# Turned first triangular blocks on VectorE instead of through HBM, and an earlier block store

## The chip, the core and the metric

The kernel runs on one NeuronCore of a Trainium2 chip. TensorE (PE in the profile) does the matrix products, VectorE (DVE) and ScalarE (ACT) the element-wise work, GpSimd (POOL) small work and some DMA, and SyncE (SP) streams the weights. The metric is the device time of one launch, in microseconds (us), lower is better; the median over several runs counts.

## What is computed

One layer of a bidirectional encoder for 256 tokens of width 2048, in float32: a SwiGLU feed-forward, then two mixers side by side (a bidirectional RWKV-7 recurrence and differential attention) that gates merge, then a second feed-forward. The parts that matter here:

```python
proj = u @ w_in[i]
rw_seg, q, k, v, gate_a, gate_b = jnp.split(proj, col_split, axis=-1)
y_a = rwkv7_branch(rw_seg, ...)        # a scan over time, both directions
y_b = diff_attention_branch(q, k, v, ...)
merged = jax.nn.sigmoid(gate_a) * (y_a @ w_branch_a[i]) + jax.nn.sigmoid(gate_b) * (y_b @ w_branch_b[i])

def step(S, inp):                      # the scan of rwkv7_branch
    sa = -jnp.einsum('dbhij,dbhj->dbhi', S, kk_t)
    S = S * w_t[..., None, :] + sa[..., :, None] * (kk_t * a_t)[..., None, :] + v_t[..., :, None] * k_t[..., None, :]
    return S, jnp.einsum('dbhij,dbhj->dbhi', S, r_t)
```

The kernel runs the scan in chunks of 64 tokens. Each chunk needs the inverse of a unit triangular 64x64 matrix, `z`. There are 128 such matrices (16 heads, 2 directions, 4 chunks).

## The kernel before

**Slots.** Every large product is cut into slots. A slot is 512 KB of weights (256 rows by 512 columns). SP loads it to `raw`, ACT rounds it to `whi` (L534), DVE makes the remainder `wlo` (L1031), and PE multiplies it in 12 matmuls of 512 columns (L1667 to L1669). The ring has 4 places. ACT may write slot n only when PE has finished slot n-4, and SP may load slot n only when DVE is done with slot n-4.

**The gate stage.** The gates' product has 64 slots, k = 0 to 63, and other work is woven into it by hand: each engine has its own list of what it does after which slot. On ACT and DVE the list runs four slots ahead of PE's, since these engines prepare slots that PE reaches later. So what DVE does after `wlo` of slot 54 belongs to the time in which PE is at slot 50 or 51. The woven work is the attention (scores on PE, `maxima` on DVE, `exps` on ACT, `maps` on DVE, transposed maps and products with the values on PE, `squares` on ACT, `head_squares` and `norm_heads` on DVE, transposed heads on PE, `store_heads` from POOL) and the triangular inverses. `S_AT` says after which slot of PE the scores of attention step n come, n = 0 to 7, and the numbers in brackets below are these n, or the group g = 0 to 3 of two steps.

**The inverses.** DVE inverts the two 32x32 diagonal blocks of all 128 matrices by elimination in `z`, where a partition holds a matrix (`step`, L1394 and L1396), in the gaps of slots up to about the 42nd. POOL stores `z` to HBM (`z_dram`, L2338) and reads it back in four groups g of 16 chunks as `zs`, where a partition holds a row of the matrices (`load_z`, L2325). The remaining block is the product of the first diagonal block with the off-diagonal one and the second diagonal block: PE does `vz_products(g)` (L1935) after slot 51 + 2g and `z12_products(g)` (L1943) after slot 52 + 2g, and ACT moves the results (L825, L833). The stationary operand of `vz_products` is `z1t`, the first diagonal block turned over. Before, DVE wrote the turned blocks to `zt` (L1398), POOL stored them (L2340) and read them back in the other layout (L2344).

**POOL's queue** is one list in order: a wait in it holds all that stands behind it. `rms(1)` waits for DVE, `store_heads(1)` for ACT's copy of the heads, `load_z(g)` for PE to have used slot 45 + 2g.

Of the kernel before, what the change touches and what calls it, by code (L numbers as in the profile page):

```python
# [38 lines left out]
ALU = mybir.AluOpType  # L39
# [3 lines left out]
P = 128  # L43
# [6 lines left out]
RING = 4  # L50
# [5 lines left out]
RW = 1024  # L56
# [7 lines left out]
C = 64  # L64
NC_ = T // C
HC = C // 2
NM = 2 * NPAIR
# [46 lines left out]
def layer(nc, a, out):  # L114
# [85 lines left out]
    def scratch(name, shape):  # L200
        return nc.dram_tensor(name, shape, F32).ap()
# [8 lines left out]
    z_dram = scratch("z_dram", (2, NM, NC_, C, C))  # L210
    beta_dram = scratch("beta_dram", (P, NM, T))
    yt_dram = scratch("yt_dram", (P, 8, T))
    z1t_dram = scratch("z1t_dram", (2, NM, NC_, HC, HC))

    ctx = ExitStack()
    with ctx:
        def sem(name):
            return ctx.enter_context(nc.semaphore(name))

        def sb(scope, name, shape, dt=F32):  # L220
            return scope.enter_context(nc.sbuf_tensor(name, shape, dt))
# [14 lines left out]
        def room(*names):  # L236

            scope = ExitStack()
            tiles = [sb(scope, *n) for n in names]
            return scope, tiles  # L240
# [9 lines left out]
        def ffn_room(tag):  # L250
# [28 lines left out]
        s_e.close()  # L279
        s_rk.close()  # L280

        s_z, (z, zt, ra, rb, xin, mx, su, os_, _, gst_g, yts) = room(
            ("z", [P, C + 1, C]), ("zt", [P, HC * HC]), ("ra", [P, RW]), ("rb", [P, RW]), ("xin", [P, 4, RW]),
            ("mx", [P, 2, 2]), ("su", [P, 2, 2]), ("os_", [P, 16]), ("z_gap", [P, 168]),
            ("gst_g", [P, 2, NT, CW]), ("yts", [P, 4, P]))
        qk = [xin[:, i, :].rearrange("p (n t) -> p n t", t=P) for i in range(4)]
# [50 lines left out]
        bon_in, bon_mm, bon_st, bon_out, v1_in = (sem(n) for n in ("bon_in", "bon_mm", "bon_st", "bon_out", "v1_in"))  # L337
        n_mm, n_st, z_in, z_done, z_out = (sem(n) for n in ("n_mm", "n_st", "z_in", "z_done", "z_out"))
        n_out = [sem("n_out0"), sem("n_out1")]
        z1t_out, z1t_in, vz_mm, vz_ready, z12_mm, z12_ready = (  # L340
            sem(n) for n in ("z1t_out", "z1t_in", "vz_mm", "vz_ready", "z12_mm", "z12_ready"))
        ZG = 4
        xin_in = zs_in = [sem(f"xin_zs_in{g}") for g in range(ZG)]
        ZS_LANDED = 16 + 32
        PER_ZG = NM * NC_ // ZG
        GATE_SLOTS = p_gate.chunks * p_gate.slots
        Z_FIRST, Z_LAST, ZS_AT, VZ_AT, Z12_AT, ZG_STEP = 13, 41, 46, 51, 52, 2
# [669 lines left out]
        def _(dve):  # L1017
            links = [0]

            def link(ins):  # L1020
                links[0] += 1
                ins.then_inc(dve_link, 1)
                dve.wait_ge(dve_link, links[0])

            V = nc.vector

            def split_lo(p):
                def slot(n, i, u, j):
                    s = slot_of(p, u, j)
                    dve.wait_ge(hi_ready, n + 1)  # L1030
                    V.tensor_tensor(wlo[:, s, :, 0:p.width], raw[:, s, :, 0:p.width],  # L1031
                                    whi[:, s, :, 0:p.width].bitcast(F32), ALU.subtract).then_inc(lo_ready, 1)
                return slot
# [243 lines left out]
            for c in range(7):  # L1277
# [3 lines left out]
                for i in range(4 if c < 6 else 0):  # L1281
# [7 lines left out]
                    if c == 1 and i == 3:  # L1289
                        dve.wait_ge(lora_act, GS_SPLIT + 2)  # L1290
                        r = slice(32, 64)
# [89 lines left out]
            def steps_by(k):  # L1381

                share = min(max(k - Z_FIRST, 0) / (Z_LAST - Z_FIRST), 1)
                return next(i for i in range(HC + 1) if sum(STEP_WORK[:i]) >= share * sum(STEP_WORK) - 1)

            def step(s):
                n = HC - 1 - s
                if s == 0:
                    dve.wait_ge(z_in, 16)
                    link(V.memset(ones, 1.0))  # L1390
                elif n:
                    prod = ra[:, 0:2 * s * n].rearrange("p (k c t) -> p k c t", k=2, c=s)
                    rest = zd[:, :, 0:s, s + 1:HC]
                    link(V.tensor_tensor(prod, zd[:, :, 0:s, s:s + 1].broadcast_to((P, 2, s, n)),  # L1394
                                         zd[:, :, s:s + 1, s + 1:HC].broadcast_to((P, 2, s, n)), ALU.mult))
                    link(V.tensor_tensor(rest, rest, prod, ALU.add))  # L1396
                else:
                    V.tensor_copy(zt[:, :].rearrange("p (t c) -> p t c", c=HC),  # L1398
                                  z[:, 0:HC, 0:HC].rearrange("p c t -> p t c")).then_inc(z_done, 1)

            def ends(m):

                if m >= 2:
                    dve.wait_ge(gh_mm, 2 * (m - 1))
                at = 1 + 3 * NC_ * NM + NC_ * (m % 2)
                V.tensor_tensor(q[:, at:at + NC_, :], q[:, 0:1, scan_columns(m)].broadcast_to((P, NC_, C)),
                                pend[:, m, :].unsqueeze(2).broadcast_to((P, NC_, C)), ALU.mult).then_inc(dd_ready, 1)

            def maxima(n):

                dve.wait_ge(sc_mm, n + 1)
                for s in range(2):
                    last = V.tensor_reduce(mx[:, :, s], ps[:, 4 + s, :].rearrange("p (v t) -> p v t", v=2), AX.X, ALU.max)
                link(last)
                V.tensor_scalar(mx[:, :, :], mx[:, :, :], -0.125, None, ALU.mult).then_inc(mx_ready, 1)
# [16 lines left out]
            def head_squares(g):  # L1432
                dve.wait_ge(pv_sq, g + 1)
                V.tensor_scalar(os_[:, 4:8], os_[:, 0:4], 1.0 / P, SUBLN_EPS, ALU.mult, ALU.add).then_inc(pv_ms, 1)

            def norm_heads(g):
                dve.wait_ge(pv_rs, g + 1)
                V.tensor_tensor(ov[:, :, :], ps[:, 6, :].rearrange("p (v i) -> p v i", v=4),
                                os_[:, 8:12].unsqueeze(2).broadcast_to((P, 4, P)), ALU.mult).then_inc(yb_ready, 1)

            slots = p_gate.chunks * p_gate.slots
            for k in range(slots):
                if k == slots - 2:
                    dve.wait_ge(z12_mm, ZG)
                    ends(0)
                    ends(1)
                if k >= RING:
                    split_lo(p_gate)(p_gate.n0 + k, 0, k // p_gate.slots, k % p_gate.slots)
                if k in TURN_AT:
                    i = TURN_AT.index(k)  # L1450
                    dve.wait_ge(xin_in[i], 16)
                    rope(V, xin[:, i, :], i % NT, ra[:, :], rb[:, :], roped, i, dve)
                for n in range(8):
                    if k - RING == S_AT[n]:
                        maxima(n)
                    if k - RING == S_AT[n] + 2:
                        maps(n)
                    if n % 2 and k - RING == S_AT[n] + PV_LATE:
                        head_squares(n // 2)
                    if n % 2 and k - RING == S_AT[n] + PV_LATE + 1:  # L1460
                        norm_heads(n // 2)
                for s in range(steps_by(k), steps_by(k + 1)):
                    step(s)

# [193 lines left out]
        def _(pe):  # L1658
# [265 lines left out]
            def vz_products(g):  # L1924
                if g == 0:
                    pe.wait_ge(n_st, NM)
                    pe.wait_ge(z1t_in, 32)
                    pe.wait_ge(qk_turned, 4)
                pe.wait_ge(zs_in[g], ZS_LANDED)
                if g:  # L1930
                    pe.wait_ge(z12_ready, g)
                for j in range(PER_ZG):
                    for h in range(2):
                        a_, b_, mc = slice(C * h, C * h + HC), slice(C * h + HC, C * (h + 1)), PER_ZG * g + j
                        last = mm(ps[b_, 7, j * HC:(j + 1) * HC], zs[a_, mc, HC:C], z1t[a_, mc, :], start=True, stop=True)  # L1935
                last.then_inc(vz_mm, 1)
# [248 lines left out]
        def _(pool):  # L2185
# [3 lines left out]
            def link(ins):  # L2189
                links[0] += 1  # L2190
                ins.then_inc(pool_link, 1)
                pool.wait_ge(pool_link, links[0])
# [123 lines left out]
            def store_heads(g):  # L2316
                hs, t = 4 * (g % 2), g // 2
                pool.wait_ge(yb_out, g + 1)
                pool.dma_start(yt_dram[:, hs:hs + 4, t * P:(t + 1) * P], yts[:, :, :]).then_inc(yt_out, 16)

            def load_z(g):
                pool.wait_ge(slots_used, p_gate.n0 + ZS_AT + ZG_STEP * g)
                ms = slice(NM // ZG * g, NM // ZG * (g + 1))
                for h in range(2):
# [8 lines left out]
            store_heads(0)  # L2333
            store_gates([3])
            rms(1)
            store_heads(1)
            pool.wait_ge(z_done, 1)
            pool.dma_start(z_dram.rearrange("h m c s t -> (h m c) (s t)"),  # L2338
                           z[:, 0:C, :].rearrange("p c t -> p (c t)")).then_inc(z_out, 16)
            pool.dma_start(z1t_dram.rearrange("h m c s t -> (h m c) (s t)"), zt[:, :]).then_inc(z1t_out, 16)  # L2340
            store_gates([4])
            pool.wait_ge(z1t_out, 16)
            for h in range(2):
                pool.dma_start(z1t[C * h:C * h + HC, :, :], z1t_dram[h].rearrange("m c s t -> s (m c) t")).then_inc(z1t_in, 16)  # L2344
            pool.wait_ge(z_out, 16)
            load_z(0)
            load_z(1)
# [106 lines left out]
```

## Time and profile before

| | us |
|---|---|
| median of 3 runs | 2337.79 (2337.22 to 2338.06) |
| time of the profiled execution | 2336.86 |
| its span, first to last instruction | 2335.1 |
| PE busy | 2303.0 (99%) |
| DVE busy | 1503.2 (64%) |
| ACT busy | 1119.6 (48%) |
| DMA, mean over the span | 193 GB/s |

PE is the engine that decides, so the table is read as: what does PE wait for, and how long. All times below are us from the start of the span. The gate stage's last third, in which the inverses lie, runs from about 1196 to 1296.

### The profile page before, as it was taken

The page shows a single profiled execution, that of the slowest core. Times are in us where ns is not written, and L with a number is a line of the kernel's source. Part 1 is how long each engine was busy: PE and PEld are TensorE (multiplying, and loading weights), DVE is VectorE, ACT ScalarE, POOL GpSimd, SP SyncE. Part 2 cuts the span into 40 slices and gives each one's busy share as a digit, 9 for nine tenths or more (in the row PEclk, how much of TensorE's full clock was granted, in tenths as well). Part 3 has the DMA queues.
Part 4 walks back from the last instruction along what each step waited for, and adds up shares of the span by engine and source line. Part 5 has one row for each costly group of instructions (what it writes and reads, how often), then busy time and mean ns, then how long its engine had stood idle before and what let it go on. Part 6 is the DMA issues. An engine that isn't in the chain of part 4 may idle for free.

```text
span 2335.1 us, 32570 instructions
## 1 busy us (share of the span) xinstructions
PE 2303.0 (99%) x12207; PEld 1883.9 (81%) x12207; DVE 1503.2 (64%) x2022; ACT 1119.6 (48%) x1504; POOL 133.5 (6%) x209
## 2 busy tenths in 40 slices
PE   9999999999999999999999999999999999999998
PEld 7888888888887778777887877887888888888886
DVE  5766754566756665997974556756676665476665
ACT  6454443444445665554566444445444443444443
POOL 1000000000000101222002210000000000000000
PEclk9999999999999999999999999999999999999999
DMA  8666666666665756668767314675766656666654
GB/s 266 192 196 195 191 196 193 189 197 192 190 195 180 238 164 190 197 202 281 222 211 216 129 46 147 217 246 153 225 192 194 195 192 193 194 190 197 193 194 145
DMA packets 229970, 451.51 MB, mean 193 GB/s; under 512 B 23436, under 2 KB 26272, under 8 KB 228448
## 3 DMA queue, kind: packets, MB, share of 16 engines
q1 hardware_dynamic: 208016, 399.88, 55.8%
q0 software_dynamic: 11600, 45.31, 5.7%
q10 hardware_dynamic: 10240, 4.76, 0.8%
q8 instruction: 76, 1.25, 0.2%
q14 instruction: 38, 0.31, 0.0%
HBM read 427.35 MB, written 22.54 MB: 193 GB/s over the span
## 4 chain that ended last, share of the span: by engine, by line
PE 91%; DVE 4%; DMA 2%; ACT 2%; issue 1%; POOL 0%; ACTq 0%; DVEq 0%; SPq 0%; POOLq 0%
PE ps L1667 28%; PE ps L1669 27%; PE ps L1668 27%; DVE wlo L1031 1%; PE ps L2037 1%; DMA raw<-in_w_in 1%; PE ps L2093 1%; PE ps L2078 1%; PE ps L2038 1%; PE ps L2079 1%; DMA xin<-dif_dram 1%; DVE h L1120 0%; DMA n_dram<-nst 0%; PE ps L2063 0%; DVE gh L1543 0%
## 5 line engine op out<-in xcount | busy, mean ns | idle before, releaser
L1031 DVE TENSOR_TENSOR wlo<-raw,whi 128x1024 fp32r<-128x1024 f32 (+1 forms) x760 | 929.2, 1227 | 676.3 <-ACT whi L534 671.3
L534 ACT ACTIVATE whi<-raw 128x1024 fp32r<-128x1024 f32 (+1 forms) x760 | 801.0, 1058 | 940.4 <-PE ps L1669 892.8
L1667 PE MATMUL ps<-whi,uhi 128*128 128x512 f32 (+1 forms) x2272 | 895.5, 394 | 6.6 <-DVE ulo L1070 2.5
L1668 PE MATMUL ps<-wlo,uhi 128*128 128x512 f32 (+1 forms) x2272 | 883.9, 389 | 0.0
L1669 PE MATMUL ps<-whi,ulo 128*128 128x512 f32 (+1 forms) x2272 | 883.8, 389 | 0.0
L1667 PEld LDWEIGHTS ps<-whi,uhi 128*128 128x128 f32 x2272 | 426.4, 188 | 103.9 <-issue 11.8
L1669 PEld LDWEIGHTS ps<-whi,ulo 128*128 128x128 f32 x2272 | 426.6, 188 | 89.3
L1668 PEld LDWEIGHTS ps<-wlo,uhi 128*128 128x128 f32 x2272 | 426.8, 188 | 84.1
L1667 PE MATMUL ps<-whi,hthi 128*128 128x512 f32 x704 | 273.9, 389 | 0.0
L1668 PE MATMUL ps<-wlo,hthi 128*128 128x512 f32 x704 | 273.9, 389 | 0.0
L1669 PE MATMUL ps<-whi,htlo 128*128 128x512 f32 x704 | 273.9, 389 | 0.0
L1175 DVE STREAM_TRANSPOSE hr<-hm 32x256 f32<-32x256 f32 x352 | 153.4, 436 | 5.7
L1667 PEld LDWEIGHTS ps<-whi,hthi 128*128 128x128 f32 x704 | 132.1, 188 | 27.5
L1668 PEld LDWEIGHTS ps<-wlo,hthi 128*128 128x128 f32 x704 | 132.1, 188 | 27.4
L1669 PEld LDWEIGHTS ps<-whi,htlo 128*128 128x128 f32 x704 | 132.1, 188 | 27.4
L2213 POOL DMA_DIRECT2D h_dram<-h x1 | 0.8, 751 | 711.5 <-DVE h L1120 711.5
L1543 DVE TENSOR_TENSOR gh<-ps,kc 128x512 f32<-128x512 f32 x32 | 20.6, 686 | 23.0 <-PE ps L2079 23.0
L2093 PEld LDWEIGHTS ps<-sv,gh 128*64 128x64 f32 x448 | 20.3, 136 | 13.4 <-ACT sv L963 6.2
L1164 DVE SCALAR_TENSOR_TENSOR hm<-ps,sm,sg 128x512 f32<-128x512 f32 x44 | 30.9, 743 | 0.0
L2093 PE MATMUL ps<-sv,gh 128*64 128x64 f32 x448 | 29.1, 234 | 1.3 <-DVE gh L1543 1.3
L2078 PE MATMUL ps<-mb,wt 64*128 64x128 f32 x256 | 30.1, 291 | 0.0
L732 ACT ACTIVATE ybuf<-ps 128x256 f32<-128x256 f32 (+1 forms) x28 | 10.8, 384 | 38.4 <-PE ps L1831 38.4
(309 smaller groups left out, 1419.2 us busy)
## 6 DMA issues: line engine op xcount, KB each, us to landing
raw<-in_ffn_w_gu SPq DMA_DIRECT2D x352, 512.0 KB, 4.4
raw<-in_ffn_w_down SPq DMA_DIRECT2D x176, 512.0 KB, 4.6
raw<-in_w_in SPq DMA_DIRECT2D x160, 512.0 KB, 4.0
raw<-in_w_out SPq DMA_DIRECT2D x32, 512.0 KB, 4.6
raw<-in_w_branch_a SPq DMA_DIRECT2D x16, 512.0 KB, 4.2
raw<-in_w_branch_b SPq DMA_DIRECT2D x16, 512.0 KB, 4.6
gate_dram<-gst_g POOLq DMA_DIRECT2D x8, 512.0 KB, 5.9
gbuf<-gate_dram POOLq DMA_DIRECT2D x8, 512.0 KB, 5.2
```

The costliest lines, as they stand in the source:

```text
L534: nc.scalar.activation(whi[:, s, :, 0:p.width], raw[:, s, :, 0:p.width], ACT.Copy).then_inc(hi_ready, 1)
L1031: V.tensor_tensor(wlo[:, s, :, 0:p.width], raw[:, s, :, 0:p.width], whi[:, s, :, 0:p.width].bitcast(F32), ALU.subtract).then_inc(lo_ready, 1)
L1164: last = V.scalar_tensor_tensor(out=hm[:, t, :], in0=ps[:, 2 * gu.pair(1) + t, :], scalar=rstd(e, t), in1=sg[:, t, :], op0=ALU.mult, op1=A ...
L1175: last = V.transpose(dst[:, a], src[:, r])
L1667: mm(o, at, w_, start=(j == 0 and k == 0), stop=False)
L1668: mm(o, at, l_, start=False, stop=False)
L1669: return mm(o, bt, w_, start=False, stop=(j == p.slots - 1 and k == SB - 1))
L2037: mm(o[:, 0:2 * C], beta[r, m, c * C:(c + 1) * C], q[r, at:dd + 1:dd - at, scan_columns(m)], start=True, stop=True)
L2038: last = mm(o[:, 2 * C:4 * C], q[r, at + 2, :], q[r, 0:at + 2:at + 1, :], start=True, stop=True)
L2078: mm(o, wt[r, m % 2, c, :], mb[r, m % 2, c, 0:2 * C], start=True, stop=False)
L2079: last = mm(o, ik[r, c, :], q[r, at:dd + 1:dd - at, scan_columns(m)], start=False, stop=True)
L2093: return mm(ps[rows_, 7, c * P + h * C:c * P + (h + 1) * C], gh[:, m % 2, NC_ * h + c, cols], sv[:, m % 2, c, h * C:(h + 1) * C], start=Tr ...
```

## The change

DVE no longer writes `zt`, and the store and the two reads of the turned blocks are gone. In their place a new function `turn_z1(g)` on DVE transposes the first diagonal blocks from `zs` after they have been read back, with two 32-partition transposes for each group. It stands in DVE's list after `wlo` of slot 54 + 2g and behind all attention work of that place. PE's `vz_products(g)` waits for it (`z1t_ready`). On POOL the store of `z` stands ahead of `store_heads(1)` instead of behind it.

```diff
--- before.py
+++ after.py
@@ -210,7 +210,6 @@
     z_dram = scratch("z_dram", (2, NM, NC_, C, C))
     beta_dram = scratch("beta_dram", (P, NM, T))
     yt_dram = scratch("yt_dram", (P, 8, T))
-    z1t_dram = scratch("z1t_dram", (2, NM, NC_, HC, HC))
 
     ctx = ExitStack()
     with ctx:
@@ -279,8 +278,8 @@
         s_e.close()
         s_rk.close()
 
-        s_z, (z, zt, ra, rb, xin, mx, su, os_, _, gst_g, yts) = room(
-            ("z", [P, C + 1, C]), ("zt", [P, HC * HC]), ("ra", [P, RW]), ("rb", [P, RW]), ("xin", [P, 4, RW]),
+        s_z, (z, _, ra, rb, xin, mx, su, os_, _, gst_g, yts) = room(
+            ("z", [P, C + 1, C]), ("zt_gap", [P, HC * HC]), ("ra", [P, RW]), ("rb", [P, RW]), ("xin", [P, 4, RW]),
             ("mx", [P, 2, 2]), ("su", [P, 2, 2]), ("os_", [P, 16]), ("z_gap", [P, 168]),
             ("gst_g", [P, 2, NT, CW]), ("yts", [P, 4, P]))
         qk = [xin[:, i, :].rearrange("p (n t) -> p n t", t=P) for i in range(4)]
@@ -337,8 +336,8 @@
         bon_in, bon_mm, bon_st, bon_out, v1_in = (sem(n) for n in ("bon_in", "bon_mm", "bon_st", "bon_out", "v1_in"))
         n_mm, n_st, z_in, z_done, z_out = (sem(n) for n in ("n_mm", "n_st", "z_in", "z_done", "z_out"))
         n_out = [sem("n_out0"), sem("n_out1")]
-        z1t_out, z1t_in, vz_mm, vz_ready, z12_mm, z12_ready = (
-            sem(n) for n in ("z1t_out", "z1t_in", "vz_mm", "vz_ready", "z12_mm", "z12_ready"))
+        z1t_ready, vz_mm, vz_ready, z12_mm, z12_ready = (
+            sem(n) for n in ("z1t_ready", "vz_mm", "vz_ready", "z12_mm", "z12_ready"))
         ZG = 4
         xin_in = zs_in = [sem(f"xin_zs_in{g}") for g in range(ZG)]
         ZS_LANDED = 16 + 32
@@ -1393,10 +1392,20 @@
                     rest = zd[:, :, 0:s, s + 1:HC]
                     link(V.tensor_tensor(prod, zd[:, :, 0:s, s:s + 1].broadcast_to((P, 2, s, n)),
                                          zd[:, :, s:s + 1, s + 1:HC].broadcast_to((P, 2, s, n)), ALU.mult))
-                    link(V.tensor_tensor(rest, rest, prod, ALU.add))
-                else:
-                    V.tensor_copy(zt[:, :].rearrange("p (t c) -> p t c", c=HC),
-                                  z[:, 0:HC, 0:HC].rearrange("p c t -> p t c")).then_inc(z_done, 1)
+                    added = V.tensor_tensor(rest, rest, prod, ALU.add)
+                    if n > 1:
+                        link(added)
+                    else:
+                        added.then_inc(z_done, 1)
+
+            def turn_z1(g):
+
+                dve.wait_ge(zs_in[g], ZS_LANDED)
+                ms = slice(PER_ZG * g, PER_ZG * (g + 1))
+                for h in range(2):
+                    r = slice(C * h, C * h + HC)
+                    last = V.transpose(z1t[r, ms, :], zs[r, ms, 0:HC])
+                last.then_inc(z1t_ready, 1)
 
             def ends(m):
 
@@ -1459,6 +1468,9 @@
                         head_squares(n // 2)
                     if n % 2 and k - RING == S_AT[n] + PV_LATE + 1:
                         norm_heads(n // 2)
+                for g in range(ZG):
+                    if k - RING == VZ_AT + ZG_STEP * g - 1:
+                        turn_z1(g)
                 for s in range(steps_by(k), steps_by(k + 1)):
                     step(s)
 
@@ -1924,9 +1936,9 @@
             def vz_products(g):
                 if g == 0:
                     pe.wait_ge(n_st, NM)
-                    pe.wait_ge(z1t_in, 32)
                     pe.wait_ge(qk_turned, 4)
                 pe.wait_ge(zs_in[g], ZS_LANDED)
+                pe.wait_ge(z1t_ready, g + 1)
                 if g:
                     pe.wait_ge(z12_ready, g)
                 for j in range(PER_ZG):
@@ -2333,15 +2345,11 @@
             store_heads(0)
             store_gates([3])
             rms(1)
-            store_heads(1)
             pool.wait_ge(z_done, 1)
             pool.dma_start(z_dram.rearrange("h m c s t -> (h m c) (s t)"),
                            z[:, 0:C, :].rearrange("p c t -> p (c t)")).then_inc(z_out, 16)
-            pool.dma_start(z1t_dram.rearrange("h m c s t -> (h m c) (s t)"), zt[:, :]).then_inc(z1t_out, 16)
+            store_heads(1)
             store_gates([4])
-            pool.wait_ge(z1t_out, 16)
-            for h in range(2):
-                pool.dma_start(z1t[C * h:C * h + HC, :, :], z1t_dram[h].rearrange("m c s t -> s (m c) t")).then_inc(z1t_in, 16)
             pool.wait_ge(z_out, 16)
             load_z(0)
             load_z(1)
```

DVE's queue around slots 53 to 57, before. `wlo` is the weights' remainder, `os_` and `rb<-ps,os_` are the head norms, `su` and `rb<-pex` the attention maps of step 6, `mx` the maxima of step 7.

```order
L1031 TENSOR_TENSOR wlo<-raw,whi 128x1024 [waits hi_ready]
L1438 TENSOR_TENSOR rb<-ps,os_ 128x512 [waits pv_rs]
L1422 RECIPROCAL su<-su 128x4 [waits am_t,ex_p]
L1423 TENSOR_TENSOR su<-su,sm 128x2 [waits dve_link]
L1425 TENSOR_SCALAR rb<-pex,su 128x256 [waits dve_link]
L1425 TENSOR_SCALAR rb<-pex,su 128x256
L1428 SCALAR_TENSOR_TENSOR rb<-pex,su,rb 128x256 [waits dve_link]
L1428 SCALAR_TENSOR_TENSOR rb<-pex,su,rb 128x256
L1031 TENSOR_TENSOR wlo<-raw,whi 128x1024 [waits hi_ready] x2
L1413 TENSOR_REDUCE mx<-ps 128x2 [waits sc_mm]
```

The same place in the changed kernel, where line numbers are shifted by a few:

```order
L1030 TENSOR_TENSOR wlo<-raw,whi 128x1024 [waits hi_ready]
L1447 TENSOR_TENSOR rb<-ps,os_ 128x512 [waits pv_rs]
L1431 RECIPROCAL su<-su 128x4 [waits am_t,ex_p]
L1432 TENSOR_TENSOR su<-su,sm 128x2 [waits dve_link]
L1434 TENSOR_SCALAR rb<-pex,su 128x256 [waits dve_link]
L1434 TENSOR_SCALAR rb<-pex,su 128x256
L1437 SCALAR_TENSOR_TENSOR rb<-pex,su,rb 128x256 [waits dve_link]
L1437 SCALAR_TENSOR_TENSOR rb<-pex,su,rb 128x256
L1407 STREAM_TRANSPOSE z1t<-zs 32x512 [waits xin_zs_in0]
L1407 STREAM_TRANSPOSE z1t<-zs 32x512
L1030 TENSOR_TENSOR wlo<-raw,whi 128x1024 [waits hi_ready] x2
L1422 TENSOR_REDUCE mx<-ps 128x2 [waits sc_mm]
```

The first `wlo` row is slot 54's. The two transposes of group 0 stand behind it, the head norm and the four operations on the maps, and ahead of `wlo` of slots 55 and 56.

PE's queue at the end of slot 51, before (`xin_zs_in0` is the landing of `zs`, group 0):

```order
L1667 MATMUL ps<-whi,uhi 128x512
L1668 MATMUL ps<-wlo,uhi 128x512
L1669 MATMUL ps<-whi,ulo 128x512
L1935 MATMUL ps<-z1t,zs 32x32 [waits qk_turned,xin_zs_in0,z1t_in,n_st]
L1935 MATMUL ps<-z1t,zs 32x32 x31
```

The same place in the changed kernel:

```order
L1679 MATMUL ps<-whi,uhi 128x512
L1680 MATMUL ps<-wlo,uhi 128x512
L1681 MATMUL ps<-whi,ulo 128x512
L1947 MATMUL ps<-z1t,zs 32x32 [waits xin_zs_in0,z1t_ready,qk_turned,n_st]
L1947 MATMUL ps<-z1t,zs 32x32 x31
```

Nothing moved on PE; the wait for a DMA (`z1t_in`) became a wait for DVE (`z1t_ready`).

POOL's queue, before:

```order
L2314 TENSOR_TENSOR os_<-os_,sm 128x4 [waits yb_ready,pv_ms]
L2319 DMA yt_dram<-yts 128x4x128 [waits yb_out]
L2338 DMA z_dram<-z 128x4096 [waits z_done]
L2340 DMA z1t_dram<-zt 128x1024
L2307 DMA gate_dram<-gst_g 128x2x512 [waits pair_free1]
L2344 DMA z1t<-z1t_dram 32x64x32 [waits z1t_out]
L2344 DMA z1t<-z1t_dram 32x64x32
L2325 DMA zs<-z_dram 64x16x64 [waits slots_used,z_out]
```

And in the changed kernel:

```order
L2326 TENSOR_TENSOR os_<-os_,sm 128x4 [waits yb_ready,pv_ms]
L2349 DMA z_dram<-z 128x4096 [waits z_done]
L2331 DMA yt_dram<-yts 128x4x128 [waits yb_out]
L2319 DMA gate_dram<-gst_g 128x2x512 [waits pair_free1]
L2337 DMA zs<-z_dram 64x16x64 [waits slots_used,z_out]
```

The store of `z` moved ahead of the heads' store, and three transfers are gone.

## Rows read from the trace of the kernel before

**Rows 1.** The page's busy time of the engines.
```profile
PE 2303.0 (99%) x12207; PEld 1883.9 (81%) x12207; DVE 1503.2 (64%) x2022; ACT 1119.6 (48%) x1504; POOL 133.5 (6%) x209
```
**Rows 2.** Busy time in one stretch: PE, PEld, DVE, ACT, POOL, clock, DMA share, GB/s.
```profile
1196.00:1296.00 100.00, 95.67 (x935) 77.53 (x935) 46.41 (x76) 58.37 (x115) 20.43 (x27) 1.00 0.77 231
```
**Rows 3.** PE's timeline: start, duration, operation, idle before and its releaser.
```profile
1230.85 0.60 PE L1977 MATMUL ps<-kc,rb 128*128 128x128 f32 x4
...
1237.08 2.05 PE L1988 MATMUL ps<-va,amt 128*128 128x128 f32 x16 [1.60 <-ACT amt L861]
1238.88 0.47 PE L1667 MATMUL ps<-whi,uhi 128*128 128x512 f32 x1
...
1244.54 1.20 PE L1935 MATMUL ps<-z1t,zs 32*32 32x32 f32 x64
...
1250.13 0.66 PE L1995 MATMUL ps<-kc,rb 128*128 128x128 f32 x4 [1.45 <-DVE rb L1438]
...
1264.90 1.20 PE L1935 MATMUL ps<-z1t,zs 32*32 32x32 f32 x64
1269.97 1.20 PE L1943 MATMUL ps<-zs,q 32*32 32x32 f32 x64 [0.93 <-ACT q L825]
```
**Rows 4.** ACT's timeline around slots 53 and 54.
```profile
1241.93 1.06 ACT L534 ACTIVATE whi<-raw 128x1024 fp32r<-128x1024 f32 x1 [4.91 <-DMA raw<-in_w_in]
1242.90 0.26 ACT L870 ACTIVATE rb<-ps 128x128 f32<-128x128 f32 x1
...
1247.15 2.01 ACT L534 ACTIVATE whi<-raw 128x1024 fp32r<-128x1024 f32 x2
```
**Rows 5.** DVE's timeline: the end of `z`, slot 54, and the maps.
```profile
1197.91 1.08 DVE L1398 COPY zt<-z 128x1024 f32<-128x1024 f32 x1
...
1248.25 1.23 DVE L1031 TENSOR_TENSOR wlo<-raw,whi 128x1024 fp32r<-128x1024 f32 x1 [3.92 <-ACT whi L534]
...
1251.04 0.88 DVE L1428 SCALAR_TENSOR_TENSOR rb<-pex,su,rb 128x256 f32<-128x256 f32 x2
...
1264.06 0.88 DVE L1428 SCALAR_TENSOR_TENSOR rb<-pex,su,rb 128x256 f32<-128x256 f32 x2
```
**Rows 6.** Groups by line, 100 to 2300 us: busy, mean ns, idle before.
```profile
L1175 DVE STREAM_TRANSPOSE hr<-hm 32x256 f32<-32x256 f32 x336 | 146.4, 436 | 5.4
```
**Rows 7.** POOL's timeline, its DMA issues.
```profile
1201.72 1.02 POOL L2314 TENSOR_TENSOR os_<-os_,sm 128x4 f32<-128x4 f32 x1 [19.80 <-DVE os_ L1434]
...
1214.79 0.56 POOL L2338 DMA_DIRECT2D z_dram<-z  x1
1215.34 0.55 POOL L2340 DMA_DIRECT2D z1t_dram<-zt  x1
...
1225.61 2.16 POOL L2344 DMA_DIRECT2D z1t<-z1t_dram  x2 [9.01 <-DMA z1t_dram<-zt]
1227.76 3.30 POOL L2325 DMA_DIRECT2D zs<-z_dram  x4
```
**Rows 8.** Busy time in three stretches; the last two columns are DMA.
```profile
1214.80:1223.00 8.20, 8.20 (x42) 6.43 (x41) 6.50 (x9) 4.32 (x11) 1.80 (x3) 1.00 0.99 377
...
1230.90:1241.40 10.50, 8.90 (x52) 7.07 (x52) 4.68 (x6) 4.34 (x6) 0.16 (x1) 1.00 1.05 197
...
1202.80:1213.00 10.20, 10.20 (x49) 8.41 (x48) 2.79 (x5) 8.58 (x15) 0.00 (x0) 1.00 0.38 121
```
**Rows 9.** Weight loads of L496: the one issued at 1228.9, then those of 1240:1250.
```profile
DMA to landing us min/median/max: 13.0/13.0/13.0
...
DMA to landing us min/median/max: 5.0/6.5/7.9
```
**Rows 10.** PE's timeline at the start; then stretches at its end (clock third last).
```profile
1.73 3.78 PE L1801 MATMUL ps<-hthi 128*128 128x512 f32 x8 [1.73 <-DVE hthi L1203]
...
2325.00:2328.20 3.20, 0.27 (x2) 0.00 (x0) 3.13 (x7) 0.72 (x2) 0.00 (x0) 1.00 0.22 82
...
2328.20:2328.30 0.10, 0.00 (x0) 0.00 (x0) 0.10 (x1) 0.00 (x0) 0.00 (x0) 0.50 0.62 225
```

## The prediction, made before the changed kernel was run

> **What bounds the kernel now.** I read the page first: PE is busy for 2303.0 of the span [rows 1], so a change counts only where it alters what PE waits for. Then I cut out the stretch in which the inverses lie. From 1196 to 1296 PE is idle for 100 - 95.67 = 4.33 us [rows 2]. That is all that any repair of this stretch can give back, and it is less than 0.2% of the time (4.7 us), which is about what a measurement of this kernel can tell from no change.
>
> PE's timeline shows the idle in four pieces: 1.60 ahead of the values' product at 1237.08, 1.45 ahead of the head transposes at 1250.13, 0.93 ahead of `z12_products(2)` at 1269.97 [rows 3], and the rest, 0.35, in between. The first two come from late weights. ACT got the weights of slot 53 only at 1241.93, after 4.91 us of waiting for the DMA [rows 4]. The weight load issued at 1228.9 took 13.0 us to land, while loads of 1240 to 1250 took 5.0 to 7.9 [rows 9]. In between, from 1230.9 to 1241.4, the DMA engines were busy all the time and moved only 197 GB/s, about half of the 377 GB/s of 1214.8 to 1223 [rows 8]. That is the time of the small reads: `z1t` issued at 1225.61 and `zs` from 1227.76 [rows 7].
>
> **The change, part by part.**
>
> *The copy to `zt`* (1.08 us on DVE at 1197.91 [rows 5]) goes. PE does not wait there, so it is worth nothing, and `z` is done 1.08 earlier.
>
> *The store of `z`* moves ahead of `store_heads(1)`. POOL has done `rms(1)` at 1201.72 + 1.02 = 1202.7, and `z` is ready since 1198, so the store is issued at 1202.7 instead of 1214.79 [rows 7]. From 1202.8 to 1213 the DMA engines are busy for 0.38 of the time, which leaves 10.2 x 0.62 = 6.3 us. The store's 2 MB at 377 GB/s need 5.6 us [rows 8]. It fits.
>
> *The store and two reads of `z1t`* go: 0.5 MB at 377 GB/s are 1.4 us, and 0.5 MB of small pieces at 197 GB/s are 2.7 us [rows 8]. With the store of `z` this takes 5.6 + 1.4 + 2.7 = 9.7 us of DMA work out of the 26.6 us between 1214.8 and 1241.4.
>
> *`load_z(0)`* can start when slot 45 is done. PE is through slot 48 at 1230.85 [rows 3], and a slot takes (1244.54 - 1238.88) / 2 = 2.83 us with what lies around it or about 2.7 alone, so this is at about 1222.7, 5 us earlier than before. The weights of slot 53 can then be requested at about 1225 (ACT 1.06 and DVE 1.23 after slot 45, [rows 4, 5]), and ACT can use them when slot 49 is done, at 1237.08 - 1.60 - 0.1 = 1235.35. That leaves 10 us for a transfer that took 5.0 to 7.9 beside such reads [rows 9]. I take it that no weight is late any more.
>
> *The transposes.* The trace has transposes of 256 elements a partition at 436 ns [rows 6]; those here have 512. Bounds are 0.44 and 0.87 us each. I take 0.7 (a fixed part and a part by size), and 1.4 for the two of a group.
>
> *Where they stand.* This decides. PE wants the first turned group after slot 51. DVE makes it after `wlo` of slot 54, the head norm and the maps of step 6. Step by step, with all weights there:
> - PE starts the values' product at 1235.35 instead of 1237.08, and would be at `vz_products(0)` after 1.8 for it and 5.66 for slots 50 and 51 [rows 3]: at 1242.8.
> - ACT can start `squares(2)` when that product is through, 2.0 after its start (2.05, [rows 3]): at 1237.35. From there to its copy for slot 54 it needs 1247.15 - 1242.90 = 4.25 (squares, a table load, four exponentials, [rows 4]): at 1241.6. Slot 50 is done by then.
> - DVE starts `wlo` of slot 54 1.10 later (1248.25 against 1247.15, [rows 4, 5]): 1242.7. It needs 1251.04 + 0.88 - 1248.25 = 3.67 for it, the head norm and the maps, less a small overlap, 3.6 [rows 5]: 1246.3. Then 1.4 for the transposes: 1247.7.
> - So PE waits from 1242.8 to 1247.75, **4.95 us**, where before there was no wait.
>
> After that `vz_products(0)` is 3.2 late against 1244.54. The head transposes no longer wait their 1.45, so PE is 1.75 late there. The next turned group stands behind `wlo` of 56 and the maxima, and is ready about 1 us before PE wants it. Group 2 stands behind the maps of step 7, which ended at 1264.06 + 0.88 = 1264.94 [rows 5], while PE had begun `vz_products(2)` at 1264.90 [rows 3]. All that is tied together and shifts alike, so PE waits another 1.4 + 0.1 = 1.5 there, and the 0.93 at 1269.97 disappears. Group 3 has slack.
>
> Sum for PE: +4.95 - 1.60 - 1.45 + 1.5 - 0.93 = **+2.4 us** (rounded for 0.07 of latencies). Behind 1296 everything hangs on PE and shifts rigidly. The profiled execution would have a span of 2337.5 and a time of 2339.3, and the median, 0.9 above the profiled time before, is 2340.2.
>
> **The clock.** A wait of 4.95 us is longer than any that PE has before; the longest is 1.73, at the start. At the end of the trace PE stops at 2325.27, and the granted clock is 1.00 up to 2328.2 and 0.50 behind [rows 10]: it fell from 2.4 to 1.2 GHz 2.9 us after the last matmul. So it may well fall within the new wait. What it costs afterwards is bounded by nothing below and by the start of the kernel above, where 8 matmuls of 512 columns took 3.78 [rows 10] and at 0.235 each (24 in 5.66, [rows 3]) would have taken 1.9: a loss of 1.9. I take the whole 1.9, since the wait is the first long one. Sum +4.3, median **2342.1**. The Trainium skill, TensorE: Matmul & The Clock Gate, section "Part 1: The HAM clock gate", says that the half rate is the default and that activity releases it. By that rule a wait brings it back too; by the rows of this stretch alone (clock 1.00 throughout) it would stay at +2.4.
>
> **Rivals.**
> - *The wait, and the clock holds*: +2.4, 2340.2. For it: the clock fell only after 2.9 us of rest, so in a wait shortened by 2 us it would not.
> - *The DMA relief doesn't come*: the weights of slot 53 are as late as before, since the store of `z` now collides with weights from 1202.8, or `zs` alone makes the jam. Then the maps end where they do now, at 1251.9, the group is turned at 1253.35, and PE waits 8.8 from 1244.54. Less 1.45, plus 1.5, less 0.93: +7.9, 2345.7. It decides from the point where slot 53 lands after 1235.35; each us beyond it is a us of PE until 1241.93. Against it: 9.7 us of DMA work fewer.
> - *No effect*: the new wait and the old ones cancel, as they would if ACT's exponentials or DVE's maps ran some 2.4 us sooner than in my chain. About 2338. Against it: the chain from PE's own product to the maps is made of measured durations.
> - *Faster*: the turned blocks come in time and only the old idle goes, -4.33, 2333.5. For this DVE would have to be through at 1242.8. The chain above misses that by 5 us, and even the whole 4.33 stays inside what counts as no change; faster by more needs something beside it.
>
> **How the numbers follow.** Wait with falling clock 0.40 (of this 0.22 within 0.2% and 0.18 over it, since +4.3 lies close to 4.7); wait with held clock 0.30 (0.28 and 0.02); no relief 0.14, all slower; no effect 0.11, all same; faster 0.05 (0.03 of it over 0.2%). Together: faster 0.03, same 0.63 (0.22 + 0.28 + 0.11 + 0.02), slower 0.34. The range runs from 2339.0 (held clock with transposes of 0.44 and some latencies less) to 2345.7 (no relief). It leaves out no effect, faster, and a relief that fails together with a falling clock.
>
> **What the profile would show.** PE's wait ahead of the first `vz_products`, released by DVE's transpose, of about 5 us, and one of about 1.5 ahead of the third; no ACT wait for `raw` around slots 49 to 53; the store of `z` issued at about 1202.7; transposes of 0.6 to 0.8; no idle ahead of the values' product of group 2; and a granted clock below 1.00 right after the first wait, or not. I am wrong if DVE gets through its list before slot 54 sooner than PE's own pace lets it in my chain, if the weights are still late, or if the clock stays down for longer than at the start.

## The result, and the profile after

| | before | changed |
|---|---|---|
| median of 21 runs each, us | 2336.57 | 2340.70 |
| lowest to highest | 2333.56 to 2338.06 | 2338.77 to 2344.01 |
| span of the profiled execution | 2335.1 | 2341.3 |

The ratio is 1.0018, 95% interval 1.0012 to 1.0024: 4.1 us slower. The forecast was +4.3, with 2342.1 as the time. Its difference from 2340.7 lies mostly in the base, since the three runs of before that it started from had a median of 2337.79 and the 21 have 2336.57.

The page of the changed kernel has its busy line; against [rows 1] PE is busy for 3 us more with the same number of matmuls (x12207 in both); stretches at a lower clock, shown below, make them longer.

```profile
PE 2305.9 (98%) x12207; PEld 1887.0 (81%) x12207; DVE 1508.4 (64%) x2029; ACT 1121.7 (48%) x1504; POOL 130.9 (6%) x206
```

PE's timeline of the changed kernel shows where the time went; it answers to [rows 3]. Lines are shifted by 12, so L1947 is `vz_products` and L1955 `z12_products`.

```profile
1232.70 1.13 PE L1977 MATMUL ps<-xin 64*128 64x256 f32 x8
1236.64 1.95 PE L2000 MATMUL ps<-va,amt 128*128 128x128 f32 x16
1249.16 1.92 PE L1947 MATMUL ps<-z1t,zs 32*32 32x32 f32 x64 [5.12 <-DVE z1t L1407]
1255.85 0.60 PE L2007 MATMUL ps<-kc,rb 128*128 128x128 f32 x4
...
1272.08 1.20 PE L1947 MATMUL ps<-z1t,zs 32*32 32x32 f32 x64 [1.38 <-issue]
1276.17 1.20 PE L1955 MATMUL ps<-zs,q 32*32 32x32 f32 x64
```

There is no idle any more ahead of the values' product (1236.64), the head transposes (1255.85) and `z12_products(2)` (1276.17). In their place stand 5.12 ahead of the first turned group and 1.38 ahead of the third. The first one's releaser is DVE's transpose. The third's row says "issue", which means that the profile names no releaser. DVE's timeline shows both chains, and in the second the transposes end at 1271.98, 0.10 before PE starts:

```profile
1244.00 1.23 DVE L1030 TENSOR_TENSOR wlo<-raw,whi 128x1024 fp32r<-128x1024 f32 x1 [4.03 <-ACT whi L533]
...
1247.60 1.41 DVE L1407 STREAM_TRANSPOSE z1t<-zs 32x512 f32<-32x512 f32 x2
...
1270.57 1.41 DVE L1407 STREAM_TRANSPOSE z1t<-zs 32x512 f32<-32x512 f32 x2
```

From the start of the split of slot 54 to the start of the transposes are 3.6 us, and the two transposes take 1.41. POOL's timeline shows the moved store and the earlier reads, against [rows 7]:

```profile
1204.12 0.59 POOL L2349 DMA_DIRECT2D z_dram<-z  x1
...
1224.72 1.67 POOL L2337 DMA_DIRECT2D zs<-z_dram  x2 [7.84 <-PE ps L1681]
```

ACT waits for no weights at all between 1196 and 1300. The loads issued between 1224 and 1232 landed in 5.7 to 6.7 us, where the one of [rows 9] took 13.0:

```profile
DMA to landing us min/median/max: 5.7/6.1/6.7
```

The clock (third column from the end) in stretches around the wait, changed kernel:

```profile
1248.00:1249.00 1.00, 0.00 (x0) 0.00 (x0) 0.99 (x2) 0.00 (x0) 0.00 (x0) 0.75 0.98 207
1249.00:1250.00 1.00, 0.84 (x32) 0.87 (x34) 0.97 (x2) 0.00 (x0) 0.00 (x0) 0.50 1.18 365
...
1254.00:1255.00 1.00, 1.00 (x3) 0.72 (x3) 0.00 (x0) 0.00 (x0) 0.00 (x0) 0.50 0.00 0
1255.00:1256.00 1.00, 1.00 (x6) 0.81 (x5) 0.00 (x0) 0.00 (x0) 0.00 (x0) 0.84 0.00 0
```

PE stops at 1244.04 (1249.16 less 5.12). The clock falls at about 1248.5 to 1.2 GHz and is back at 2.4 at about 1255.3. Nearly the whole of `vz_products(0)` and slot 52 runs at half rate.

The two profiled spans differ by 6.2 us, more than the medians. 1.3 us of this were there before the stretch: the scores of step 6 start at 1232.70, against 1231.38 before. At the kernel's start PE waits for `x`, for 1.98 here and 0.85 before, and in this one execution the clock fell there too, for 3.4 us from about 9.5. The stretch from 5 to 20 us, which has 1.00 before:

```profile
5.00:20.00 15.00, 13.02 (x59) 10.28 (x58) 9.42 (x14) 10.52 (x18) 9.27 (x18) 0.89 1.06 375
```

So the experiments are read by three pieces of PE's timeline: A from the scores of step 6 to `vz_products(0)`, B from there to the head transposes of group 2, C from there to `z12_products(3)`. All are differences of start times.

| us | A | B | C | sum | against before |
|---|---|---|---|---|---|
| before | 13.16 | 5.59 | 30.25 | 49.00 | |
| changed | 16.46 | 6.69 | 30.70 | 53.85 | +4.85 |
| changed, second profile (its own run, below) | 16.43 | 6.21 | 30.62 | 53.26 | +4.26 |
| changed, third profile (of the timed runs, below) | 16.45 | 7.13 | 32.34 | 55.92 | +6.92 |
| turn a slot earlier | 11.24 | 4.00 | 30.14 | 45.38 | -3.62 |
| the same, store of `z` late | 11.60 | 3.98 | 30.16 | 45.74 | -3.26 |
| store early alone | 12.04 | 3.99 | 30.33 | 46.36 | -2.64 |
| turned blocks alone | 17.70 | 6.75 | 30.64 | 55.09 | +6.09 |
| turn ahead of the maps | 13.97 | 6.77 | 30.18 | 50.92 | +1.92 |
| the same, second profile | 13.96 | 5.59 | 30.17 | 49.72 | +0.72 |
| wait filled | 16.44 | 4.03 | 30.63 | 51.10 | +2.10 |
| wait filled, second profile | 16.45 | 3.99 | 32.25 | 52.69 | +3.69 |

B without any idle and at full clock is 4.0.

### The profile page after: what moved, and what is told of

It reads as the page before. It is cut to its first block, busy times and chain, and to the rows that moved or that the text cites. A ratio compares the mean times of both kernels' runs of the same rounds, so it can differ in the third digit from the quotient of the medians.

```text
span 2341.3 us, 32574 instructions
## 1 busy us (share of the span) xinstructions
PE 2305.9 (98%) x12207; PEld 1887.0 (81%) x12207; DVE 1508.4 (64%) x2029; ACT 1121.7 (48%) x1504; POOL 130.9 (6%) x206
## 4 chain that ended last, share of the span: by engine, by line
PE 93%; DVE 3%; DMA 1%; ACT 1%; issue 1%; POOL 0%; DVEq 0%; ACTq 0%; POOLq 0%
PE ps L1679 29%; PE ps L1681 28%; PE ps L1680 28%; PE ps L2049 1%; PE ps L2105 1%; PE ps L2090 1%; PE ps L2050 1%; PE ps L2091 1%; DVE wlo L1030 1%; DMA xin<-dif_dram 1%; DVE h L1119 0%; DMA n_dram<-nst 0%; PE ps L2075 0%; PE ps L1745 0%; DVE gh L1555 0%
```

## The experiments

**The transposes one slot earlier.** Each group stands behind the split of slot 53 + 2g.

```diff
-                    if k - RING == VZ_AT + ZG_STEP * g - 1:
+                    if k - RING == VZ_AT + ZG_STEP * g - 2:
                         turn_z1(g)
```

> The changed kernel with each group's transposes one slot earlier in VectorE's list (group 0 behind the split of slot 53 instead of 54 with its head norm and maps). Theory (the wait is only a matter of place in VectorE's list; the DMA relief is real): no PE wait ahead of the turned blocks, clock 1.00 there, idle of 1.60 and 1.45 from the kernel before gone, 0.36 and 0.93 still there. Time: before - 3.1 us, ratio to before 0.9987. Rival 1 (the blocks read back land too late for this place, so VectorE waits and holds the weight splits behind it): a wait of 2 us or more stays, time within 1 us of before. Rival 2 (the transposes themselves cost, wherever they stand): about 1 to 2 us above the theory's time.

Measured: median 2332.99 against 2336.93, ratio 0.9985 (0.9976 to 0.9994). DVE's timeline of this kernel:

```profile
1238.02 0.17 DVE L1443 TENSOR_SCALAR os_<-os_ 128x4 f32<-128x4 f32 x1 [0.58 <-ACT rb L869]
1238.10 1.41 DVE L1407 STREAM_TRANSPOSE z1t<-zs 32x512 f32<-32x512 f32 x2
1242.21 1.23 DVE L1030 TENSOR_TENSOR wlo<-raw,whi 128x1024 fp32r<-128x1024 f32 x1 [2.71 <-ACT whi L533]
```

The transposes fill a gap in which DVE waits for ACT anyway, and PE takes `vz_products(0)` at 1242.19 without a wait. So place is the whole of the transposes' cost; as work they cost nothing. The theory stands. The two idles that it removes are 3.05 us; the stretch gained 3.62 and the medians differ by 3.9, more than the 3.1 forecast. This version beats both kernels: its interval lies wholly below 1, and that of the changed kernel (1.0012 to 1.0024) wholly above.

**The store of `z` early, turned blocks still through HBM.**

```diff
 (before.py)
             rms(1)
-            store_heads(1)
             pool.wait_ge(z_done, 1)
             pool.dma_start(z_dram..., z...).then_inc(z_out, 16)
+            store_heads(1)
             pool.dma_start(z1t_dram..., zt[:, :]).then_inc(z1t_out, 16)
```

> The kernel before with one edit: the store of z ahead of the second heads; the turned blocks still go through HBM. Theory A (the jam is bytes: 5.6 us of store moved out of it are enough): ScalarE's DMA waits around slots 49 to 53 fall from 11.5 us to under 3, PE's idle of 1.60 and 1.45 goes, time = before - 3.1 us, ratio 0.9987. Theory B (the jam is the small reads, which stay): slot 53's weights still late by 3 us or more, time within 1 us of before.

Measured: 2333.42 against 2336.93, ratio 0.9987 (0.9978 to 0.9996). ACT's waits for weights between 1190 and 1300 fall to 3.3 us in two. PE's idle is 0.5 ahead of the values' product and none ahead of the head transposes. Moving one line, with nothing else, gives nearly the whole relief, and theory B is out. That the moved bytes are the reason, as theory A has it, isn't shown by this: with the move the small reads were issued earlier too (`z1t` at 1219.46 instead of 1225.61, `zs` from 1223.17 instead of 1227.76), and no run separates the two. ACT's 3.3 is also a little above the "under 3" of the theory.

**The turned blocks alone**: the changed kernel with the store of `z` behind `store_heads(1)` again (the same lines, the other way).

> The changed kernel with the store of z back behind the second heads, so the turned blocks on VectorE are the only edit left. The DMA work taken out of 1214.8 to 1241.4 is then 4.1 us (bytes and small reads of the turned blocks) instead of 9.7. Theory (store order gives the relief; without it slot 53's weights are still about 2.5 us late, and each us of that is a us of PE's wait): ScalarE waits for weights by 4 to 7 us in all, PE waits about 7.5 us for the first turned group, time = changed kernel + 2.5 (ratio to before about 1.003). Rival (the small reads were the jam): no waits for weights, PE's wait 5.1 us, time of the changed kernel, 1.0018.

Measured: 2341.98 against 2337.62, ratio 1.0019 (1.0010 to 1.0028). ACT waits for weights by 7.3 us in four, as the theory had it, but PE waits 6.05 us and not 7.5:

```profile
1247.96 1.92 PE L1947 MATMUL ps<-z1t,zs 32*32 32x32 f32 x64 [6.05 <-DVE z1t L1407]
```

Slot 53's weights came late here too (ACT's copy at 1236.51 after a wait of 2.20). But behind this copy ACT waits for the values' product in any case, until 2 us after its start at 1234.37, so about 1 us of lateness costs nothing. In time the two edits together and this one alone can't be told apart (1.0018 and 1.0019); the trace shows 0.9 us more of wait.

**The wait filled with needless matmuls**, in two series of runs, the second beside the unaltered changed kernel. It adds 18 matmuls of 512 columns to PE and throws their result away.

```diff
                 if g == 0:
                     pe.wait_ge(n_st, NM)
                     pe.wait_ge(qk_turned, 4)
+                    keep = uhi[:, 0:2, :].rearrange("p k t -> p (k t)")
+                    for _ in range(18):
+                        mm(ps[:, 7, :], uhi[:, 0, 0:P], keep, start=True, stop=True)
                 pe.wait_ge(zs_in[g], ZS_LANDED)
                 pe.wait_ge(z1t_ready, g + 1)
```

> The changed kernel with 18 needless matmuls of 512 columns into a free PSUM bank (added work, results thrown away) ahead of PE's wait for the first turned group. They take about 3.9 us of the 5.1 us wait. Theory (the idle drops the clock, and the low clock costs a further 2.5 us): clock 1.00 throughout, vz_products(0) starts where it did, from its start to the head transposes 4.1 us instead of 6.7, time = changed kernel - 2.5, about before + 1.7. Rival (the slow slot behind the wait has another cause, such as late weights): 6.7 us stays and the time is that of the changed kernel.

> The changed kernel unaltered, timed on one chip together with the next run, since the two earlier ratios (1.0018 and, with the wait filled, 1.0008) come from different calls and their intervals touch. Theory: before + 4, ratio 1.0018.

> The changed kernel with the 18 needless matmuls in PE's wait, on the same chip as the run before. Theory (the low clock costs 2 to 2.5 us): 2 to 2.5 us faster than the unaltered changed kernel beside it. Rival (the clock costs nothing in the end): within 0.5 us of it.

Measured: first series 2338.92 against 2336.93, ratio 1.0008 (0.9999 to 1.0017). Second series, all on one chip: changed kernel 2340.69 (ratio to before 1.0015, 1.0006 to 1.0024), with the wait filled 2338.81 (1.0009, 1.0000 to 1.0018), before 2337.13. PE's timeline of the first:

```profile
1240.20 4.24 PE L1942 MATMUL ps<-uhi 128*128 128x512 f32 x18
1245.48 1.20 PE L1950 MATMUL ps<-z1t,zs 32*32 32x32 f32 x64 [1.04 <-DVE z1t L1407]
1249.51 0.60 PE L2010 MATMUL ps<-kc,rb 128*128 128x128 f32 x4
```

Piece A is unchanged at 16.44, so `vz_products(0)` starts no sooner. Piece B falls from 6.69 to 4.03. A kernel with 4.2 us more of work is 1.9 us faster than the same kernel without it, so the idle itself costs again through the clock. The theory said 2 to 2.5; 1.9 is just below. The two intervals overlap, so the medians alone carry this weakly; the pieces carry it: with the wait filled B is 4.03 and 3.99 in two profiles, without it 6.69, 6.21 and 7.13.

**The transposes ahead of head norm and maps**, profiled twice.

```diff
+                for g in range(ZG):
+                    if k - RING == VZ_AT + ZG_STEP * g - 1:
+                        turn_z1(g)
                 for n in range(8):
                     if k - RING == S_AT[n]:
                         maxima(n)
...
-                for g in range(ZG):
-                    if k - RING == VZ_AT + ZG_STEP * g - 1:
-                        turn_z1(g)
```

> The changed kernel with the transposes directly behind the split of slot 54 + 2g, ahead of head norm and maps (2.5 us earlier than in the changed kernel). Theory (wait = place in the list, one for one; the clock falls only in a long wait): first wait 5.1 - 2.5 = 2.6 us with clock 1.00, no wait for group 2, 0.93 idle back at z12_products(2). Time = changed kernel - 2.5 - 1.4 + 0.9 - 2.5 = - 5.5 us, about before - 1.3. Rival (the clock has no part, or also falls in 2.6 us): - 3.0 us only, about before + 1.2.

> The kernel with the transposes ahead of head norm and maps, a second profile. PE's wait is again 2.6 us. Theory (in a wait of this length the clock falls in some executions only, by the moment at which it begins): the clock may be 1.00 here, and vz_products(0) to the head transposes then takes 4.1 us instead of 6.8. Rival (2.6 us always suffice): 6.8 again.

Measured: 2337.09 against 2336.93, ratio 0.9999 (0.9990 to 1.0008). Both profiles have the wait of 2.65 that place alone gives, no wait for group 2, and 0.93 back at `z12_products(2)`. The time lies between the theory's (before less 1.3) and the rival's (before plus 1.2). The part on the clock failed: it fell in both. In the first profile it fell within the wait, in the second two us after PE had gone back to work at 1244.30:

```profile
1246.00:1247.00 1.00, 1.00 (x5) 0.79 (x4) 1.00 (x3) 0.72 (x2) 0.00 (x0) 0.73 1.02 213
1247.00:1248.00 1.00, 1.00 (x4) 0.81 (x3) 0.86 (x1) 0.00 (x0) 0.00 (x0) 0.50 1.06 289
...
1249.00:1250.00 1.00, 1.00 (x4) 0.66 (x3) 0.00 (x0) 0.00 (x0) 0.00 (x0) 0.57 0.91 141
```

The price was 2.8 (B 6.77) the first time and 1.6 (B 5.59) the second.

**The early turn with the late store.** Both edits of the first and third experiments together.

> The transposes one slot earlier, as in the first experiment, and the store of z behind the second heads, as in the kernel before. Theory (place and store order act apart): group 0 is read back and turned by about 1241.5, so no wait ahead of it or less than 1 us, but the late weights leave 1 to 3 us of idle ahead of the values' product and the head transposes. Time between before - 2.5 and before - 0.5, ratio about 0.9993. Rival (the early turn alone carries the gain of the first experiment): 0.9985, as that one.

Measured: 2333.29 against 2337.62, ratio 0.9981 (0.9972 to 0.9990). My theory fell and the rival stands. ACT still waits 7.2 us for weights, yet PE has no idle ahead of the values' product or the head transposes; the waits end within the slack that ACT has. So store order and the removal of the turned blocks' traffic are not two halves of a gain: each alone takes the jam below the point at which PE notices.

**The changed kernel again.**

> The changed kernel unaltered, a second profile. Theory: PE's wait ahead of the first turned group is again 5.1 us, since it is fixed by the order of work, and the clock falls in it again; moment of fall and of return may differ. If the clock fell by chance only in the first profile, vz_products(0) to the head transposes takes 4.1 us here.

Measured: 2339.54 in its one run, the wait 5.12 once more, the clock low from 1244.4 to 1251.3, B 6.21. With the profile of the timed run beside it (B 7.13), three of three profiles of this kernel show the fall in this wait.

## Why the prediction was right, point by point

- *The place of the transposes decides.* Forecast 4.95 us of wait; measured 5.12, in all three profiles. The first experiment moves the same work by a slot and the wait is gone. The chain behind the number came step by step: the values' product (forecast 1235.35, measured 1236.64), the split of slot 54 (1242.7, 1244.00) and the start of the transposes (1246.3, 1247.60) are each 1.3 late, which is what this execution had lost before the stretch.
- *Duration of the transposes.* Taken as 0.7 between 0.44 and 0.87; measured 0.698 (eight, 0.691 to 0.703).
- *Group 2.* Forecast 1.5 behind DVE's transposes, measured 1.38 behind them; groups 1 and 3 had the slack foreseen.
- *The DMA relief.* Forecast: no weight late any more. Right, but for more reasons than needed. The sum of 9.7 us of work taken out of the jam is a sum of two parts that overlap in effect: the store's move alone was enough (idle 0.5 left), and with the early turn the removed traffic alone was enough (idle 0). In the rival on missing relief, the step "each us beyond 1235.35 is a us of PE" was wrong by about 1 us, as the third experiment showed: ACT waits for the values' product behind that copy.
- *The clock.* It fell, as forecast, and filling the wait undoes its price. The term was too small: 1.9 taken as the upper bound, 2.7, 2.2 and 3.1 in the three profiles (B less 4.0). So the start of the kernel was no bound above. (The granted clock is given as 1.00 there; only the pace of the matmuls, 3.78 us for eight, is that of half rate.) The rest of the sum, 2.4, came as 2.2 in the first profile: +3.30 in A, -1.59 in B less the clock's 2.69, +0.45 in C. So the stretch should be 4.4 to 5.3 longer with one fall; it shows +4.85 and +4.26 in two profiles and +6.92 in the third, where the clock fell a second time.
- *The total.* That the medians differ by 4.1, so near to the forecast 4.3, is in part luck. The clock's term was 0.3 to 1.2 too small, and the difference of the medians came out at or below the shortest of the profiled stretches (in the second series it was 3.6). Part of this may be that before loses time to the clock as well, as told below; how much of it, no run here shows.
- *The rule of the clock.* The remark that the clock would hold in a wait shortened by 2 us is refuted: with a wait of 2.65 it fell in both profiles, once within the wait and once behind it. The Trainium skill, TensorE: Matmul & The Clock Gate, "Part 1: The HAM clock gate", has as its rule that idle brings the half rate back; the trace agrees, with 0.50 from 1249 to 1255.
- *Faster* and *no effect* did not come. The reason given against "faster" held: the chain missed by 5 us.

The run-to-run spread of the kernel before goes with the clock too. Each of its 75 runs beside the experiments has its mean granted clock on record: 33 have 0.999, as the profiled one, 28 have 0.998 and 14 have 0.997. In all three series the runs with the lower clock are the slower ones:

| us, average by mean granted clock | 0.999 | 0.998 | 0.997 |
|---|---|---|---|
| first series, 33 runs | 2336.5 | 2337.3 | 2338.9 |
| second, 21 | 2336.4 | 2338.0 | 2339.8 |
| third, 21 | 2335.8 | 2337.3 | 2338.7 |

Not settled: where in the kernel the clock falls in these runs. The kernel before has idle of 1.60 and 1.45 in this same place, and kept 1.00 there in its one profile.

## What to carry to other kernels

When a transfer is replaced by work on an engine with a queue in fixed order, the duration of that work says little; look at what stands ahead of it there and at when the consumer wants it. Here 1.4 us of work behind 3.6 us of other work cost 5.1 us, and the same work in the gap one slot earlier cost nothing. When several edits relieve one jam, try each alone: one moved line (2333.42) gave about what the whole change gave at its best (2332.99). And a new idle of TensorE is to be counted with the clock that it may cost behind it.

## What the runs showed of the hardware that was not expected

- The granted clock fell at very different times after PE stopped: 4.5, 3.4 and 2.3 us in the three profiles of the changed kernel (wait 5.12), 2.1 us with the turned blocks alone (wait 6.05), 2.1 and 4.8 us in the two profiles of the kernel with a wait of 2.65, in the second of which PE had been at work again for 2.1 us when it fell. It then stayed at 0.50 for 6.8, 6.8 and 10.2 us, for 10.2 us, and for 6.8 and 3.4 us. The same wait can therefore cost 1.6 us in one execution and 2.8 in the next.
- In the third profile the clock also fell behind the wait of only 1.40 us for group 2. Ahead of this wait PE had done a whole slot of 512-column matmuls, behind it came the 64 small ones (32x32), and the clock fell at 1269.0, at their end; the next slot shows it. PE's timeline:

```profile
1267.94 1.23 PE L1947 MATMUL ps<-z1t,zs 32*32 32x32 f32 x64 [1.40 <-issue]
...
1269.69 0.63 PE L1680 MATMUL ps<-wlo,uhi 128*128 128x512 f32 x1
1270.12 0.63 PE L1681 MATMUL ps<-whi,ulo 128*128 128x512 f32 x1
```

  Matmuls of 512 columns start 0.43 us apart there and 0.23 apart at full rate. The piece from `vz_products(2)` to `z12_products(2)` was 5.62 instead of 4.09. With the wait ahead of group 0 filled, this second fall happened in one of two profiles. It isn't bound to this place: in the profile of the kernel with the turn a slot earlier, 0.50 stands for 3.4 us from about 760.8, behind a wait of 1.87 for a weight split.
- VectorE's 32-partition transposes in float32 take 436 ns for 256 elements a partition [rows 6] and 698 ns for 512.
